# Bringing the first attention section's operands in during the projection's last chunk

## What is computed

```python
qa, ka, va, qb, kb, vb, qi, ki, wi, ga, gb = project(x, g_pre_mix, w_in)      # rms_norm(x) @ w_in, 5064 columns
# A: banded attention, chunk c (64 frames) sees chunks c-2..c, 16 meta keys and a sink per head
s = where(ok, qa.ka * d**-0.5 - slope * |distance|, -inf)
o_a = softmax([s, qa.mk_a, sink]) @ [va, mv_a]
# B: an indexer scores keys, each query keeps its top 256, and 16 meta keys
score = sum_h wi[t, h] * relu(qi[t, h] . ki[s]);  o_b = softmax(top-256 scores of qb.kb, meta) @ [vb, mv_b]
mix = (sigmoid(ga) * o_a + sigmoid(gb) * o_b) @ w_o;  x = x + rms_norm(mix)
y = x + rms_norm(square(relu(rms_norm(x) @ w_up)) @ w_down)
```

## Time and profile before

| | us |
|---|---|
| median of 3 runs | 2042.55 |
| runs | 2040.95 to 2051.41 |
| the profiled execution | 2042.43 |
| its span in the trace | 2040.6 |
| PE busy in it | 1924.3 (94%) |
| DVE busy | 1178.2 (58%) |
| ACT busy | 713.2 (35%) |
| POOL busy | 578.8 (28%) |

### The profile page before, as it was taken

The page is one execution under the profiler, slowest core; times in us unless marked ns, Lnnn a source line. Parts: engine busy times, 40 slices in busy tenths (PEclk is TensorE's granted clock), DMA queues, the critical chain, the costliest instruction groups (busy, mean ns, idle before and its releaser), DMA issues. The chain is left out here.

```text
span 2040.6 us, 31131 instructions
## 1 busy us (share of the span) xinstructions
PE 1924.3 (94%) x11132; PEld 1734.4 (85%) x11132; DVE 1178.2 (58%) x2701; ACT 713.2 (35%) x1421; POOL 578.8 (28%) x444
## 2 busy tenths in 40 slices
PE   5989999999849999999997989999999999999995
PEld 5879999877638999999996868888888888888884
DVE  5249999998746566666754653333333333333337
ACT  4335544233215555655544332112122121212122
POOL 2315554133213232445611002222222222222224
PEclk9999999999977999999978999999999999999998
DMA  5423333332349134444613312111111111111104
GB/s 166 130 71 85 93 95 88 94 106 80 81 92 185 39 70 89 95 92 93 122 38 115 138 57 93 42 41 41 41 46 41 42 45 41 46 41 46 54 8 154
DMA packets 147465, 160.18 MB, mean 78 GB/s; under 512 B 35776, under 2 KB 115504, under 8 KB 147360
## 3 DMA queue, kind: packets, MB, share of 16 engines
q1 hardware_dynamic: 136416, 141.10, 26.0%
q10 hardware_dynamic: 10944, 17.72, 3.7%
HBM read 120.63 MB, written 39.27 MB: 78 GB/s over the span
## 5 line engine op out<-in xcount | busy, mean ns | idle before, releaser
L2042 PE MATMUL ps<-x2T_hi,weights 128*128 128x362 f32 (+1 forms) x1536 | 383.8, 329 | 5.3 <-DVE weights L2008 5.3
L2060 PE MATMUL ps<-weights,hid_hi 128*128 128x512 f32 (+1 forms) x1152 | 363.0, 396 | 0.0
L2042 PEld LDWEIGHTS ps<-x2T_hi,weights 128*128 128x128 f32 x1536 | 273.9, 189 | 7.0 <-DVE weights L2008 5.5
L1993 DVE TENSOR_TENSOR total<-total,ps 128x512 f32<-128x512 f32 (+1 forms) x270 | 184.9, 687 | 164.2 <-PE ps L2060 163.3
L2060 PEld LDWEIGHTS ps<-weights,hid_hi 128*128 128x128 f32 (+1 forms) x1152 | 209.6, 182 | 57.1
L2042 PE MATMUL ps<-x2T_lo,weights 128*128 128x362 f32 (+1 forms) x768 | 253.1, 330 | 0.0
L1978 DVE TENSOR_TENSOR hidden<-hidden 128x362 f32<-128x362 f32 (+1 forms) x96 | 51.6, 537 | 311.6 <-ACT hidden L1951 311.6
L2060 PE MATMUL ps<-weights,hid_lo 128*128 128x512 f32 (+1 forms) x576 | 228.1, 396 | 0.0
L869 DVE MATCH_REPLACE8 score<-top,score 128x1024 f32<-128x1024 f32 (+6 forms) x224 | 207.2, 930 | 0.0
L865 DVE MAX8 top<-score 128x8 f32<-128x1024 f32 (+6 forms) x224 | 203.1, 937 | 1.9
L1911 POOL TENSOR_TENSOR weights<-down_raw,weights 128x512 fp32r<-128x512 f32 x64 | 83.0, 1296 | 419.6 <-ACT weights L1942 419.6
(11 more groups left out here) (188 smaller groups left out, 3618.6 us busy)
## 6 DMA issues: line engine op xcount, KB each, us to landing
w_raw<-in_w_in ACTq DMA_DIRECT2D x64, 256.0 KB, 3.0
up_raw<-in_w_up SPq DMA_DIRECT2D x64, 256.0 KB, 2.8
down_raw<-in_w_down SPq DMA_DIRECT2D x64, 256.0 KB, 2.6
q_raw<-q_scr SPq DMA_DIRECT2D x30, 512.0 KB, 8.1
gates<-gate_scr SPq DMA_DIRECT2D x34, 256.0 KB, 4.7
x_in<-in_x_prompt SPq DMA_DIRECT2D x16, 512.0 KB, 4.7
gate_scr<-stage SPq DMA_DIRECT2D x32, 256.0 KB, 3.1
q_scr<-stage SPq DMA_DIRECT2D x40, 181.0 KB, 3.0
```

Source lines behind the costliest of these rows:

```text
L1993: dve.tensor_tensor(out, out, ps[:r, UP_BANKS + g % DOWN_BANKS, :], ALU.add).then_inc(added, 1)
L2042: last = pe.matmul(ps[:, g % UP_BANKS, 0:n], a[:, k, fs], b, start=(k == 0 and i == 0), stop=(k == KT - 1 and i == 2))
L2060: last = pe.matmul(ps[:r, UP_BANKS + g % DOWN_BANKS, :], a, b[:, f, cols], start=(f == 0 and i == 0), stop=(f == FT - 1 and i == 2))
```

## The change

The memory map is turned around: the projection's xT lies right above the first 32 KB of each partition, and its weights, now one tile `w` of four quarters (a hi and a lo one for even and for odd chunks), lie above it. The unrounded and the rounded keys lie over the two quarters that the last chunk doesn't use, and over `w_raw`. The first 32 KB hold `v_a_p`, `v_a_s`, `v_b_p`, `v_b_s` and a tile of its own for the first section's split queries, `q_st_first`; the raw ones, `q_raw3`, lie over the indexer's `q_raw`, `q_st`, `dist` and first `score` slot. So in the last chunk:

- SP loads the prompt keys with 9 DMAs for 12 (the meta keys for both halves in one) and behind them the first section's queries (2 DMAs for 4). ACT issues the sample keys' loads, 10 for 16, behind its first evacuation.
- PE turns key groups from the second matmul group on, four at a time.
- POOL sets the rows of `v_a_p` when all keys are turned, ahead of the sample keys' lo halves. SP then issues the 15 loads of `v_a_p` (26 before: the 16 for the meta rows are now 5), 8 behind store 6 and 7 behind store 7.
- ACT splits the first queries' hi half behind evacuation 7, POOL the lo half at its list's end.

What stood behind the last matmul and isn't among these goes to `attention`: SP's list at its head is four late masks, 4 loads of `v_b_p`, the wait for the masks, queries of section 1, `dist_b`, gates, 9 loads of sample values, 13 copies, queries of section 2. POOL sets the remaining value rows there. PE waits for `v_b_p` at section 1 and for the sample's values at the sample's first unit.

The core of the diff:

```diff
@@ projection, SP @@
+            def load_prompt_keys():
+                for i, cols in enumerate(KEY_COLS):
+                    src = t_scr[0:N_PROMPT, cols].rearrange("(j p) d -> p j d", p=P)
+                    for half in range(2):
+                        sp.dma_start(raw["raw_p"][:, :, i, half], src).then_inc(prompt_loaded, 16)
+                    src = t_scr[N_QUERY:N_TOK, cols]
+                    sp.dma_start(raw["raw_m"][:, i], src.unsqueeze(1).to_broadcast([N_META, 2, HD])).then_inc(prompt_loaded, 16)
...
             for ch in range(1, N_CH):
                 if ch == LAST:
                     sp.wait_ge(added, IDX_HEADS * len(INDEX_TILES))
-                    load_keys()
+                    load_prompt_keys()
+                    load_first_queries()
                 for g in range(len(groups_of(ch))):
                     store(ch, g)
+                    if ch == LAST and g == VALUES_AT:
+                        sp.wait_ge(value_rows_set, len(ROWS))
+                        load_values(0)
+                    if ch == LAST and g == VALUES_AT + 1:
+                        load_values(1)
...
-            sp.wait_ge(group_done, GROUP_BASE[N_CH])
-            for piece in range(2):
-                load_first_queries(slice(8 * piece, 8 * piece + 8), kv["q_first"][piece])
-            sp.wait_ge(value_rows_set, VALUE_SETS)
-            for dst, src in value_loads(kv, t_scr, cache_v_a, cache_v_b, cache_meta):
-                sp.dma_start(dst, src).then_inc(values_loaded, 16)
-            for i in LATE_MASKS:
-                store_mask(i + 2, INDEX_TILES[i])
             all_stored(N_CH - 1)
@@ projection, ACT @@
+            def first_queries_hi():
+                act.wait_ge(q_first, 32)
+                act.wait_ge(kt_turned, PROMPT_GROUPS)
+                st, loaded = FIRST_QUERIES(slice(0, P))
+                act.activation(st, loaded, ACT.Copy).then_inc(q_first_hi, 1)
...
+                    if ch == LAST and g == 0:
+                        load_sample_keys()
                     if ch == LAST:
                         for j in key_groups_at(g):
                             copy_keys(j)
+                    if ch == LAST and g == VALUES_AT + 1:
+                        first_queries_hi()
@@ key_groups_at @@
-        return range(min(3 * g, len(GROUPS)), min(3 * g + 3, len(GROUPS)))
+        first = max(0, 4 * (g - 1))
+        return range(min(first, len(GROUPS)), min(4 * g, len(GROUPS)))
@@ projection, POOL @@
+            pool.wait_ge(kt_turned, len(GROUPS))
+            for rows in ROWS:
+                pool.memset(rows, 0.0).then_inc(value_rows_set, 1)
...
-            pool.wait_ge(group_done, GROUP_BASE[N_CH])
-            for rows in sink_rows(kv):
-                pool.memset(rows, 0.0).then_inc(value_rows_set, 1)
...
+            pool.wait_ge(q_first_hi, 1)
+            st, loaded = FIRST_QUERIES(slice(HD, P))
+            pool.tensor_tensor(st, loaded, st.bitcast(F32), ALU.subtract)
@@ attention, SP @@
+                for n in range(MASKS - SCORES, MASKS):
+                    t = INDEX_TILES[n - 2]
+                    w = N_META + keys_seen(t)
+                    sp.dma_start(dist_scr[t, 0:tile_rows(t), 0:w], kv["score"][:tile_rows(t), mask_slot(n), 0:w])\
+                      .then_inc(mask_stored[mask_slot(n)], 16)
+                for dst, src in B_VALUES:
+                    sp.dma_start(dst, src).then_inc(b_values_loaded, 16)
+                for n in range(MASKS - SCORES, MASKS):
+                    sp.wait_ge(mask_stored[mask_slot(n)], 16 * (n // SCORES + 1))
                 load_q(1)
-                for n in range(MASKS - SCORES, MASKS):
-                    sp.wait_ge(kv["mask_stored"][mask_slot(n)], 16 * (n // SCORES + 1))
                 for i in range(2):
                     load_dist(i)
                 for i in range(2):
                     load_gates(i)
+                sp.wait_ge(late_rows_set, len(LATE_SETS))
+                for dst, src in SAMPLE_VALUES:
+                    sp.dma_start(dst, src).then_inc(s_values_loaded, 16)
@@ attention, PE @@
-                    if u in (0, 4):
-                        pe.wait_ge(q_first_lo, 1 + u // 4)
...
-                        pe.wait_ge(kv["values_loaded"], 16 * VALUE_LOADS)
+                        pe.wait_ge(kv["values_loaded"], 16 * A_VALUES)
+                    if u == SECTION_END[0]:
+                        pe.wait_ge(late_rows_set, len(LATE_SETS))
+                        pe.wait_ge(b_values_loaded, 16 * len(B_VALUES))
```

More of the change, by code:

```diff
@@ L446, in attention_layout @@
 def attention_layout(nc):
[L449 to L457, removed]
+    return place(nc, ("q_st_first", [P, 2, HEADS, CHUNK], F32R), ("v_a_p", [P, SAMPLE_BLOCK, 2, 2 * COL], F32),
+                 ("v_a_s", [P, 2, 2 * COL], F32), ("v_b_p", [P, 9, COL], F32), ("v_b_s", [P, 9, COL], F32),
+                 FOOT, ("wo_raw", [P, KT, D], F32), ("pt", [P, PT, 9, P], F32), ("probs", [P, 3, N_META + N_QUERY], F32),
+                 ("merged", [P, 2, D // 2], F32),
+                 FOOT + X_BYTES, ("gates", [P, 2, 2, D // 2], F32), ("mixed", [P, 2, 2, D // 2], F32),
+                 ("q_st3", [P, 2, 2, HEADS, CHUNK], F32R), KEYS_FROM, *[(n, shape, F32R) for n, shape in KEYS],
+                 Q_RAW_AT, ("q_raw3", [P, 2, HEADS, P], F32), ("dist_b", [P, 2, N_META + N_QUERY], F32),
+                 ("neg", [P, 2, 2 * PAIRS], F32), ("neg_part", [P, 2, 2], F32), ("inv", [P, 2, QUAD], F32))
@@ L1093, in meta_values @@
     def meta_values(blocks, col):
-        for i in range(blocks[1]):
-            tile, row = divmod(col, P)
-            out.append((va[row:row + N_META, blocks[0] + 3 * i, tile, VALUES], t_scr[meta, cols_a]))
+        (first, count), (tile, row) = blocks, divmod(col, P)
+        src = t_scr[meta, cols_a].unsqueeze(1).to_broadcast([N_META, count, 2 * HD])
+        out.append((va[row:row + N_META, first:first + 3 * count - 2:3, tile, VALUES], src))
     for blocks in ((2, 5), (3, 5), (4, 4), (0, 1), (1, 1)):
@@ L1150, in attention @@
         SECTION_END = [max(u for u in range(UNITS) if ALL[u][0] == s) + 1 for s in range(len(SECTIONS))]
+        SAMPLE_FROM = min(u for u in range(UNITS) if SECTIONS[ALL[u][0]][0] == SAMPLE_TILE)
         STEPS = UNITS + 4
@@ L1259, in load_q @@
                     r = tile_rows(t)
-                    if s == 2:
-                        sp.wait_ge(q_first_lo, 2)
                     if s >= 3:
@@ L1398, in exp @@
                                    scale=-1.0).then_inc(exped, 1)
-                st, loaded = queries(slice(0, P), 0)
-                for piece in range(2):
-                    heads = slice(8 * piece, 8 * piece + 8)
-                    act.wait_ge(q_first[piece], 32)
-                    act.activation(st[:, heads], loaded[:, heads], ACT.Copy).then_inc(q_first_hi, 1)
                 for u in range(STEPS):
```

170 lines of the change are left out of this document (94 added, 76 removed).

## The result

| | before | after |
|---|---|---|
| median of 4 runs each, taken together | 2046.98 us | 2021.07 us |
| lowest and highest | 2040.95, 2051.59 | 2019.63, 2021.31 |
| the profiled execution | 2042.43 | 2021.29 |
| its span | 2040.6 | 2019.5 |

The account below looks back on a forecast made before the run. SP's row of DMA issues held the barrier, making PE wait 29.7 us before attention; with DVE last instead, the first score comes 30.0 us earlier: 2042.43 - 30.0 = 2012.4 us, range 2006 to 2019.

Parts of the forecast that it names:

- The gap: PE's 29.7 us wait before attention's first score goes; DVE holds the barrier at 585.20, first score 585.95, 30.0 us earlier.
- PE's end: PE's last projection matmul ends at 577.5 instead of 586.28, by 6.8 us of wait and 2.0 of half clock.
- it also loses the wait of 6.8 us: Last projection chunk: PE no longer waits for meta keys, needed 5.54 us later with three fewer 0.52 us issues ahead.
- rival B: Another engine is last at the barrier, or section 1's queries are late; 3 us late gives 2015.4; chance 0.15.
- Section 0 at 0.50: Attention's first section stays at half clock and takes 22.6 us, so section 1's first score is due at 608.5.
- rival A: The clock doesn't stay down in section 0; section 1's queries then limit the extra gain to 2.9 us: 2009.5; chance 0.12.
- Section 1's queries: Behind the barrier, POOL has them ready at 605.6, 2.9 us before they are due; slack was 9.9 us.
- All later stages are shifted alike: Every stage after section 0 moves earlier by the same amount; named as a sign that the forecast is right.
- From section 1 on, nothing is changed: Attention from section 1 onward and everything later adds no term to the 30.0 us gain.
- The foundation of the sum: Whole program: the profiled 2042.43 us, 0.1 less than the median, less 30.0 gives 2012.4 us; chance 0.68.
- Rival C: Half clock outlasts section 0; if it covers section 1, 43 us more against 30 gained: 2055; chance 0.02.
- Rival D: Another wait, such as values landing late, holds attention's first units for most of 30 us: about 2035; chance 0.03.

Follow-up runs that it names:

- the bridge: 16 matmuls with discarded result behind PE's last projection group, added to the changed kernel with two extra matmuls per unit in tile 0's and the sample's sections: 2004.99 us.
- the filler: Two more 208-column matmuls per unit in tile 0's and the sample's sections, overwritten by the real scores: 2036.64 us on the kernel before, 2007.22 on the changed one.

## Why the prediction was right or wrong

**The gap: right.** DVE's chain kept its place (584.91, forecast 585.20), and the first score came at 586.16, forecast 585.95. In eight of ten profiles of the changed kernel and its variants DVE holds the barrier, and its wait there is 0.32 us, as in that of 2018.87 us.

**PE's end: mis-sized, with little effect on the time.** Forecast 577.5, measured 582.2. The step was "it also loses the wait of 6.8 us", worked out from one group later and three issues fewer. The three issues saved nothing, the nine took 9.0 us in place of twelve in 7.6, and 3.6 us of the wait stayed, and with it a part of the half clock. In the two other profiles of the changed kernel the wait was 2.8 and 3.2. It did cost a little: with PE late, SP's last store landed behind DVE's mask, and DVE waited 1.25 us in place of 0.32. In one more profile of the changed kernel (2022.99 us) it is 1.61. This is rival B's first half, for 0.9 and 1.3 us of its 3.

**Section 0 at 0.50: right in its size, with reservations.** 22.2 us, forecast 22.6; section 1's first score 608.34, forecast 608.5. The reason given, the idle time ahead of it, isn't what decides alone: with most of it filled by the bridge the clock fell too, and in one profile it came back within section 0 although PE had been idle for 5.9 us ahead of it. That case, rival A, was worth 3.4 us, forecast 2.9.

**Section 1's queries: right.** 8.66 us from issue to POOL's start, forecast 8.6; ready at 606.3, forecast 605.6, so 2.0 us of slack were left of 9.9.

**"All later stages are shifted alike": the step that failed**, and with it "From section 1 on, nothing is changed". True of the work, and of the time wherever the clock does the same: 29.3 us at each section from 662 to 970. It took for granted that the clock does the same over the same work. The term of the sum that was missing is the light stretch, 58.4 us for 49.2; with the filler, which held the clock at 1.00, it was 44.1 in both kernels.

**The foundation of the sum failed with it.** 2042.43 was set against the median of three, with the sentence that they "spread 1.6 us below their middle and more above it". The "more above" was 2051.41, one execution in three, 9 us off. That is no scatter around a value but a second value: 31 of 56 executions have it. A forecast from the lower group alone is some 10 us too low for the other. 2051.4 - 30.0 = 2021.4 belonged in the range; it is where the first four executions came out. The gain of 30.0 itself compares well with 32.0 and 32.4 within the groups; that the means of all executions are 30.2 apart is in part luck, since they mix the groups in different shares. Where the 2 us beyond it come from can be seen in the pair of upper-group profiles (2052.46 and 2018.87, 33.6 apart). The first score is 30.9 apart (616.19 and 585.29), the sample's B section 31.2, the first matmul of `output_mix` 31.5 (1103.47 and 1071.95) and PE's last matmul 33.6 (2027.71 and 1994.10). So 2.1 us arise in `output_mix` and `mlp`, which the change doesn't touch, and there too it is the clock: it came back 10.6 us behind the first matmul of `output_mix` in the one and 7.6 in the other, and 5.1 against 3.6 us behind the first of `mlp` at L2042 (L2095 after), by stretches of 2 us. These 2.1 us are not the change's.

**Rival C, the half clock outlasting section 0 by most of section 1: it didn't happen.** Stretches of the run after, in the columns of above:

```profile
605.00:610.00 5.00, 5.00 (x23) 4.77 (x22) 2.81 (x11) 1.53 (x4) 1.31 (x1) 0.50 1.22 208
610.00:615.00 5.00, 5.00 (x34) 4.66 (x33) 3.81 (x12) 2.56 (x4) 0.00 (x0) 0.86 0.60 131
```

The clock is back some 3 us behind section 1's first score. In the run before it was back 1.1 us behind it, which is why the shift of 30.2 us at section 1's start (638.57 to 608.34) is 29.3 at the next. This place varies as well: 4.3 us in the second profile of the kernel before, 2.8 and 4.4 in the other two of the changed one, with 53.7 to 54.5 us for section 1 where the first profile of the kernel before had 52.9. The profile that the sum was built on was the fortunate one here too.

**Rival D, another wait at the first units: it didn't happen.** From 586 to 640 PE's only wait besides the barrier is 0.2 us for ACT. Its price was also misadded: 20 us on top of 2012.4 are 2032, not 2035.

## What to carry to other kernels

Where the times shown for a kernel lie in two heaps, find out which heap the profile is from before anything is subtracted from it, and forecast both. A stretch where PE is counted as busy all the time but the granted clock is 0.50 is a stretch whose length can vary with no change to the code; such a stretch is best compared by the time from its first to its last instruction. A few extra matmuls there, in banks that are overwritten anyway, can pay: here they took the light stretch from 49.2 or 57.8 us to 44.1. When an end is moved to another engine's end, ask what share of the slack behind it is left: here the queries behind the barrier went from 9.9 us of slack to 2.0, and became the bound as soon as the clock was up.

## What the runs showed of the hardware

- The place at which the granted clock falls from 1.00 (2.4 GHz) to 0.50 (1.2 GHz) within the same work is not fixed: in 1010 to 1020 in one execution of the kernel before, in 1000 to 1010 in another. The earlier one costs 8.6 to 9.4 us (57.8 to 58.6 in four profiles, for 49.2). With more matmuls there the clock didn't fall and the stretch took 44.1.
- The place at which it comes back isn't fixed either: 1.1 to 4.4 us behind section 1's first score in five profiles, worth up to 1.5 us of section 1.
- PE at 0.50 for some 50 us while counted as 10.00 busy of 10, in tile 0's sections, and 5.00 of 5 in section 0, shows that this count doesn't tell the clock. The Trainium skill, page "TensorE: Matmul & The Clock Gate", section "Part 1: The HAM clock gate", says that sustained matmul activity releases the throttle. The trace agrees at section 1's start and in the streams with the filler; in the light stretch (0.50 for 50 us) and in most profiles of section 0 (0.50 for 22) matmuls without a counted gap didn't release it. Whether there are gaps between these small matmuls that the count leaves out, no row shows.
- A DMA issue is not of a fixed length: 0.36 to 1.36 us for one on SP in the kernel before, where six transfers of 256 KB are on their way, and up to 2.9 for a pair in the changed one. Twelve issues took 7.6 us; nine, for the same bytes, 7.6 to 9.0.
